# A one-core hybrid decoder step: in the decode attention, the matmul that spreads a unit's maxima is issued behind the value products of the unit ahead

## What is computed

```python
def mla_sample(x, ckv_pool, kpe_pool, page_table, ...):
    ckv_past = ckv_pool[page_table].reshape(B, past, MLA_KV_LORA)      # 4096 x 256
    kpe_past = kpe_pool[page_table].reshape(B, past, MLA_ROPE)         # 4096 x 32
    q_lat = jnp.einsum("bthn,chn->bthc", q_nope, w_uk)
    s_past = jnp.einsum("bthc,bkc->bhtk", q_lat, ckv_past) + jnp.einsum("bthr,bkr->bhtk", q_pe, kpe_past)
...
    s = jnp.concatenate([s_past.astype(jnp.float32), s_new], axis=-1) * scale
    p = jax.nn.softmax(s, axis=-1).astype(c_kv.dtype)
    o_lat = jnp.einsum("bhtk,bkc->bthc", p[..., :past], ckv_past) + jnp.einsum("bhtk,bkc->bthc", p[..., past:], c_kv)
    o = jnp.einsum("bthc,chv->bthv", o_lat, w_uv).reshape(B, T, MLA_HEADS * MLA_VDIM)
    return o @ w_o, c_kv, k_pe
```

## Time and profile before

| | us |
|---|---|
| median of 3 runs | 1651.08 |
| lowest and highest | 1649.51, 1653.77 |
| the profiled execution, its own time | 1653.67 |
| its span in the profile | 1651.8 |
| mean granted clock of PE in it | 0.949 of full speed |
| decode stage, first scores to last latent | 283 to 422 |

### The profile page before, as it was taken

One profiled execution on the slowest core, in us unless ns is written; L12 is line 12 of the kernel. 1 busy time (PEld: TensorE's weight loads), 2 busy tenths in 40 slices (PEclk: granted clock), 3 DMA queues, 4 the chain that ended last, 5 costly groups with the idle time before them and its releaser, 6 DMA issues.

```text
span 1651.8 us, 28361 instructions
## 1 busy us (share of the span) xinstructions
PE 1509.5 (91%) x12159; PEld 1397.5 (85%) x12159; DVE 689.2 (42%) x991; ACT 471.6 (29%) x882; POOL 611.9 (37%) x276
## 2 busy tenths in 40 slices
PE   6878887888899899998999989998879989999898
PEld 6766663555799899998999989997669989999898
DVE  4756664787254300232122475214667420034112
ACT  4225544333242211121231110103633221122221
POOL 2302212442346633555333342321014654356441
PEclk9979996999899999999999999988979999999999
DMA  4235742876144535443334555445932543535221
GB/s 150 72 111 167 256 157 69 312 292 223 57 149 139 193 128 190 140 152 127 137 143 154 173 192 166 161 141 179 326 133 72 184 153 128 203 128 178 102 77 52
DMA packets 124075, 258.81 MB, mean 157 GB/s; under 512 B 7264, under 2 KB 104688, under 8 KB 117712
## 3 DMA queue, kind: packets, MB, share of 16 engines
q1 hardware_dynamic: 117840, 219.75, 38.9%
q0 software_dynamic: 6144, 37.75, 6.2%
HBM read 249.88 MB, written 95.58 MB: 209 GB/s over the span
## 4 chain that ended last, share of the span: by engine, by line
PE 80%; DVE 9%; issue 3%; ACT 3%; DMA 2%; POOL 1%; SPq 1%; DVEq 0%; POOLq 0%; ACTq 0%
PE ps L513 21%; PE ps L517 21%; PE ps L514 21%; PE ps L790 4%; PE ps L702 2%; DMA dv<-q_scratch 1%; DVE sq L1660 1%; PE ps L930 1%; ACT sc L2180 1%; PE ps L739 1%; PE ps L713 1%; PE ps L811 1%; DVE KT L1492 1%; PE ps L893 1%; PE ps L973 1%
## 5 line engine op out<-in xcount | busy, mean ns | idle before, releaser
L2232 POOL TENSOR_TENSOR whl<-wraw,whl 128x2048 fp32r<-128x2048 f32 (+3 forms) x127 | 447.6, 3533 | 602.9 <-ACT whl L1888 602.9
L513 PE MATMUL ps<-hA,whl 128*128 128x260 f32 x1248 | 339.7, 292 | 16.5 <-POOL hA L2232 11.1
L514 PE MATMUL ps<-hA,whl 128*128 128x260 f32 x1248 | 334.6, 288 | 0.0
L1888 ACT ACTIVATE whl<-wraw 128x2048 fp32r<-128x2048 f32 (+3 forms) x127 | 185.9, 1485 | 481.3 <-PE ps L517 398.2
L513 PE MATMUL ps<-uT,whl 128*128 128x260 f32 x1024 | 273.6, 288 | 16.8 <-POOL uT L2232 16.8
L514 PE MATMUL ps<-uT,whl 128*128 128x260 f32 x1024 | 270.8, 285 | 0.0
L513 PEld LDWEIGHTS ps<-hA,whl 128*128 128x128 f32 x1248 | 243.7, 195 | 18.0 <-issue 11.5
L517 PE MATMUL ps<-hA,whl 128*128 128x260 f32 x1248 | 257.6, 289 | 0.0
L514 PEld LDWEIGHTS ps<-hA,whl 128*128 128x128 f32 x1248 | 244.2, 196 | 0.1
L513 PEld LDWEIGHTS ps<-uT,whl 128*128 128x128 f32 x1024 | 196.7, 192 | 17.6 <-issue 17.6
L517 PE MATMUL ps<-uT,whl 128*128 128x260 f32 x1024 | 209.7, 287 | 0.0
(11 more groups left out here) (290 smaller groups left out, 2004.0 us busy)
## 6 DMA issues: line engine op xcount, KB each, us to landing
out_ds<-in_state SPq DMA_DIRECT2D x32, 2047.0 KB, 10.5
wraw<-in_w_up SPq DMA_DIRECT2D x32, 1024.0 KB, 5.6
wraw<-in_w_down SPq DMA_DIRECT2D x32, 1024.0 KB, 5.1
wraw<-in_w_qkv SPq DMA_DIRECT2D x18, 1024.0 KB, 6.9
out_ds<-in_state SPq DMA_DIRECT2D x8, 2044.0 KB, 12.3
dv<-in_state SPq DMA_DIRECT2D x36, 256.0 KB, 6.1
dv<-q_scratch SPq DMA_DIRECT2D x6, 1024.0 KB, 7.2
wraw<-in_w_omla SPq DMA_DIRECT2D x4, 1024.0 KB, 11.3
```

The costliest lines, as they stand in the source:

```text
L513: pe.matmul(ps[:, 2 * u + a, 0:HALF], hi(k), rhs(k, 0)[:, c], start=first, stop=False)
L514: pe.matmul(ps[:, 2 * u + a, 0:HALF], hi(k), rhs(k, 1)[:, c], start=False, stop=False)
L1888: ins = act.activation(dst(0), src, ACT.Copy)
L2232: return pool.tensor_tensor(dst, src, hi.bitcast(F32), ALU.subtract)
```

## The change

In the loop of PE's stream, `spread_max(u)` is called behind `unit_values(u - 1)` and not in front of it. Nothing else is edited.

```diff
             for u in range(NU + 2):
                 if u < NU:
                     unit_scores(u)
-                    spread_max(u)
                 if 1 <= u <= NU:
                     unit_values(u - 1)
+                if u < NU:
+                    spread_max(u)
                 if u >= 3 and u % 2:
                     turn_latent((u - 3) // 2)
                 if u >= 2 and u % 2 == 0:
```

## The result

The changed kernel took 1662.01 us (median of 10 runs, 1657.26 to 1669.52), the kernel before 1650.33 us beside it (10 runs, 1646.30 to 1653.77). The ratio is 1.0079, 95% interval 1.0060 to 1.0098: slower by some 12 us. The forecast was 1646.6 us in a range of 1644.0 to 1650.6.

What follows compares the result with a forecast made beforehand. PE, busy 91% of a 1651.8 us span, was taken as the bound. Odd gaps (-5.1) and the stage's end (+0.6) summed to -4.5 us, taking the median of 1651.08 to 1646.6 us, range 1644.0 to 1650.6.

Steps and rivals of the forecast that it cites:

- Odd units, 0.85 us each: Six gaps of odd units 3 to 13: value products start as scores end, next scores 0.85 us sooner, 5.1 us off.
- first rival: Odd units: PE overlaps both kinds of product, the key transpose limits, each gap gains 0.92 us; 1646.0 us, chance 0.20.
- The gaps behind even units unchanged: Even units and unit 1, eight gaps: no gain, because PE still waits for rowsw before L821, or for keys in unit 1.
- End of the stage, 0.6 us lost: Unit 15: L797 comes 1.02 us later with no key transpose as cover, so last value products start 0.6 us later.
- Queued behind the new wait: L797 now also waits for L811's placed probabilities: at most 0.1 us wait in even units, 0.5 us spare in odd.
- stretched maxima: Rival: DVE's maximum over the scores slows while PE writes another PSUM bank; 1652.1 us if its time doubles, chance 0.07.
- gathers: Rival: DMA cannot give the 306 GB/s the new pace wants, so nothing is won inside the stage; 1651.7 us, chance 0.08.

Runs made afterwards that it cites:

- e3_fill_128: The changed kernel plus five unread 128 x 128 matmuls between L797 and L821 in even steps 2 to 14; time against before 0.9984 (0.9963 to 1.0004).

## Why the prediction was wrong, step by step

- **Odd units, 0.85 us each:** right in kind, with the size of the first rival. Without a fall the odd gap is 7.47 us in e3_fill_128, 0.93 under before. The next scores there start 2.72 us after the transpose of their keys (312.88 against 310.16), so the floor of the first rival (0.92) is what limits, by a little: PE's own row would end some 0.03 us sooner, as L797 to L831 takes 0.24 us and not the 0.31 that was put in. L811 starts 0.04 to 0.07 us before the modelled end of L790 (315.42 against 315.48), as assumed. The Trainium skill (TensorEngine Tiling (Array Packing), Tiling Modes) says that a change of tiling mode drains the engine; this trace fits that, but a start next to a modelled end doesn't prove it. (Where the prediction says that max_rows "has been written for over a second", a microsecond is meant.)
- **The gaps behind even units unchanged:** right, 8.02 and 8.03 us. The wait ahead of L821 was forecast at 1.2 us and measured at 1.17.
- **End of the stage, 0.6 us lost:** right in mechanism and size (0.53). The term left out that these products could run slow: 1.7 us more in the changed kernel (3.62 for 1.93).
- **Queued behind the new wait:** harmless, as said; in the changed kernel L797 stands behind L811 without a wait of its own in the steps shown.
- **The step that failed** is the one on even units: "Nothing." I wrote that the idle time "comes back in front of L821", priced it by its length, and left every L790 at 4.11 us. The runs showed 5.79 us for L790 in seven odd units (4 to 7 in the repeats), 11.8 us in all. Idle time has a second price: what it does to the clock of the work behind it. The granted clock of 1.00 in the earlier trace rows was read as a constant of the stage. The row of 292.36 shown above was in the trace; the window of 283 to 300 us in the earlier trace rows, with its clock of 0.79, stood in the prediction as evidence on DMA only.
- **The rivals:** stretched maxima and gathers fell: L1535, now L1536, is 0.42 us as before, and DMA moved 309 GB/s over a pair at the pace of 15.49 us in e3_fill_128, over the 306 that was asked. The Trainium skill (PSUM — Partial Sum Buffer, Specifications (TRN2)) speaks of ScalarE with VectorE when it promises parallel access without bank collisions; for DVE reading while PE writes another bank it is this trace, by that 0.42, that shows no stretch. None of the rivals was the clock, though the Trainium skill (TensorE: Matmul & The Clock Gate, What's actually happening) says that the clock granted is set by how busy PE has been recently. By that rule a longer idle stretch would have been a rival with a price of 1.68 us per unit; the traces agree that it can fall, and also show that it need not.

## What to carry to other kernels

Before gathering short waits of PE into one longer one, price the wait twice: by its length, and by what the matmuls behind it cost at half clock, taken from a row of the same kernel that follows a longer wait. Shorter total idle time can lose: here 0.8 us less per pair of units went with 1.7 us more for each slow score. Where a wait can't be removed, leave wide work in the middle of it (the kernel before does, with the value products between its two waits), and take the half of a reordering that makes no long gap: behind in odd units alone it was 0.3 to 0.5% faster than before in three comparisons. And take more than one profile: the same program showed from 4 to 7 falls.

## What the runs showed that I had not expected

- The clock fell to half after a stretch of 2.1 us without wide matmuls, of which 1.17 us were idle, stayed there for 3.4 us, and the fall began 0.1 to 1.3 us into the scores that followed. Scores of 4.11 us took 5.79.
- The same stretch in the same program was followed by a fall in 7, 6, 5 and 4 of 7 units in four profiles.
- Products of 8 columns in the gap did not prevent it in 2 of 7 units; with two or five products of 128 columns there was no fall in 28 units of four profiles.
- Falls in a row came 17.07 us apart against a pair of 17.18 us, so their place in the scores moved by 0.11 us per pair until the row broke off.
- What decides whether a given stretch is followed by a fall is open in general: by these runs its length and its place in time both matter (none of 7 at 1.7 us; 2, 3 or 4 to 7 of 7 at 2.1 us, by the order; 8 of 8 at 2.7 us), and no run set the place by itself.
